# Two units of the modulated projections taken from rows without the norm's factor

## The chip, the cores and the metric

The program runs on one core of one Trainium2 chip. The metric is the device time of one execution in microseconds. Five engines share the work: TensorE (PE, matrix products into PSUM banks; PEld is its weight load), VectorE (DVE), ScalarE (ACT), GpSimd (POOL), and SyncE (SP), which issues most of the transfers.

## The reference, cut to what matters

A residual stream x of 512 tokens by 1024 features goes through mixer a, mixer b, and then a second block, whose entry is the place of this change:

```python
mod = c_act @ ada_w[l] + ada_b[l]
shift, scale, gate = jnp.split(mod, 3, axis=-1)
h = rms_norm_2(x, norm_g[l]) * (1.0 + scale[:, None, :]) + shift[:, None, :]
p = h @ w_in[l]
```

`rms_norm_2` divides each token by the root of its mean square and multiplies by the gain. The modulation (shift, scale, gate) depends on `c` alone, not on the token. So for one unit of 128 columns W of `w_in`, with r the token's factor and g = norm_g * (1 + scale):

p = r * ((x * g) @ W) + shift @ W

The first term can be formed without r, and multiplied by it afterwards; the second is one number for each column. Both versions of the kernel compute the same p.

## The kernel before, in words

The activations lie feature-major: 8 rows (k = 0..7), each a tile of 128 features by 512 tokens. Each product is exact to about fp32 by splitting both sides in a high and a low part: high is a rounded copy written by ScalarE (`HH`, `wh`), low is the difference (`HL`, `wl`). A product of one row with one weight block is three matmuls (low row with high weights, high row with low weights, high with high; `split_product`, L321 to L323). A unit is one block of 128 output columns, that is 8 rows by 3 matmuls into one PSUM bank.

The program is a chain of stages, each a block of one instruction list per engine; between two stages `retire` (L140) clears the semaphores and makes all engines meet. The order within a stage is written out by hand, engine by engine, and kept by semaphores.

Three stages matter:

- Mixer a ends, and mixer b (`attention_layer`, layer b) begins, at 650 to 653 us. This seam already has the form that the change gives to the next seam: the last output units of a write x times the gain (without r) and its high rows; b starts with `raw_two` (L679): two units from those rows, 32 matmuls with the high rows, then 16 with the low rows. In their time the sum of squares is finished (L1000, L691), r is formed (L779, L781), the rows are multiplied by r (L1008), split again (L787, L1017), and the two banks are multiplied by r (`scale_unit`, L997).
- Mixer b's tail: eight output units m = 0..7, 24 matmuls each (L663). VectorE adds the residual (L1188), ScalarE squares each new row (L937), VectorE sums the squares (L309). After the last unit come the sum over features (L756, L758), then Ln and Exp for r (L939, L941), and 20 idle products on TensorE (L761) that keep it at work.
- `modulated_projections` (L1959): units ckv, 4 of qi, ki (0 to 5), and a small one, wi. VectorE forms the scale (L2100) and the eight rows x * scl * r (L2105), ScalarE adds the shift and rounds (L2064), VectorE writes the low rows (L2109). TensorE runs `first_two` (L332): 10 idle products, 32 matmuls with high rows (L339, L340), 16 with low rows (L344); then unit 2 (L321 to L323), in whose middle it makes the sum of squares for the ckv unit's own norm (L2051), which waits for ScalarE's square of bank 0 (`s_lsq`, L2073); then wi, and units 3 to 5. The weights of unit 2 are loaded by SyncE at the start of the stage, rounded by ScalarE (L2060) and their low part is made by GpSimd (L2088).

## Time and profile before

| | us |
|---|---|
| median of 3 runs | 1581.86 |
| lowest and highest of them | 1580.75, 1583.53 |
| the profiled execution, its own time | 1582.13 |
| its span in the trace | 1580.3 |

The span is what the profile shows of the program; 1.8 us of the profiled execution's time lie outside of it. Times in the trace are counted from the span's start. Every row is from that one execution. The granted clock is 1.00 for TensorE at 2.4 GHz and 0.50 at 1.2 GHz. Matmuls overlap, so the distance of two starts, not the length of one, says what a matmul costs.

### The profile page before, as it was taken

How to read it: one execution, taken by the hardware profiler on the slowest of the kernel's cores; microseconds unless marked ns; L12 is line 12 of the kernel's file. 1: busy time of each engine (PE TensorE's matmuls, PEld its weight loads, DVE VectorE, ACT ScalarE, POOL GpSimd, SP SyncE). 2: the span in 40 equal slices, each digit the busy share in tenths (PEclk: the TensorE clock that was granted, in tenths of full speed). 3: DMA queues.
4: the chain of work that ended last, by engine and by line, in shares of the span. 5: the costliest groups of instructions: out<-in, count | busy, mean ns of one | idle time of the engine just before them, and what ended most of it. 6: DMA issues, size and time to landing. Idle time of an engine off the chain costs nothing. (4 is left out here: it accounts for less than half of the span.)

```text
span 1580.3 us, 29922 instructions
## 1 busy us (share of the span) xinstructions
PE 1520.1 (96%) x11664; PEld 1221.9 (77%) x11664; DVE 815.9 (52%) x1931; ACT 783.8 (50%) x1578; POOL 779.6 (49%) x474
## 2 busy tenths in 40 slices
PE   7999999999999999989999999999998998999997
PEld 5888787878888887767777777676777886778886
DVE  5145455464545456835444324189656654274545
ACT  4653637363544545666566643346765532442222
POOL 4734436262625343465654543335777651565651
PEclk9999999999999999999999999999999999999999
DMA  6423132232414130445544214331100001433331
GB/s 155 116 75 111 54 98 80 80 95 65 121 41 122 41 110 28 104 141 152 147 142 127 70 51 105 96 81 54 48 23 3 4 17 29 107 85 103 93 94 54
DMA packets 239413, 131.26 MB, mean 83 GB/s; under 512 B 28678, under 2 KB 233550, under 8 KB 239256
## 3 DMA queue, kind: packets, MB, share of 16 engines
q1 hardware_dynamic: 231736, 114.35, 26.2%
q10 hardware_dynamic: 7536, 14.98, 3.3%
q8 instruction: 94, 1.54, 0.4%
q14 instruction: 47, 0.39, 0.1%
HBM read 126.88 MB, written 2.43 MB: 82 GB/s over the span
## 5 line engine op out<-in xcount | busy, mean ns | idle before, releaser
L1674 POOL TENSOR_TENSOR w_low<-a_w_raw,w_high 128x1024 fp32r<-128x1024 f32 x70 | 172.9, 2472 | 56.7 <-ACT w_high L1560 56.7
L321 PE MATMUL a_proj<-h_low,w_high 128*128 128x512 f32 x488 | 196.4, 402 | 1.2 <-POOL h_low L1692 1.2
L323 PE MATMUL a_proj<-h_high,w_high 128*128 128x512 f32 x488 | 192.0, 393 | 0.0
L322 PE MATMUL a_proj<-h_high,w_low 128*128 128x512 f32 x488 | 191.0, 391 | 0.0
L1687 POOL TENSOR_TENSOR a_sq_low<-a_sq,a_sq_high 128x512 fp32r<-128x512 f32 x48 | 63.0, 1313 | 247.1 <-ACT a_sq_high L1584 247.1
L949 POOL TENSOR_TENSOR w_low<-b_w_raw,w_high 128x1024 fp32r<-128x1024 f32 x40 | 97.4, 2439 | 89.6 <-ACT w_high L772 89.6
L321 PE MATMUL b_proj<-h_low,w_high 128*128 128x512 f32 x288 | 116.1, 403 | 1.4 <-POOL h_low L988 0.8
L323 PE MATMUL b_proj<-h_high,w_high 128*128 128x512 f32 x288 | 113.1, 393 | 0.0
L322 PE MATMUL b_proj<-h_high,w_low 128*128 128x512 f32 x288 | 112.5, 391 | 0.0
L321 PEld LDWEIGHTS a_proj<-h_low,w_high 128*128 128x128 f32 x488 | 91.7, 188 | 23.6 <-issue 1.4
L323 PEld LDWEIGHTS a_proj<-h_high,w_high 128*128 128x128 f32 x488 | 91.7, 188 | 20.7
L322 PEld LDWEIGHTS a_proj<-h_high,w_low 128*128 128x128 f32 x488 | 91.8, 188 | 19.0
L1601 ACT ACTIVATE a_probs<-a_probs,a_stat 128x256 f32<-128x256 f32 x128 | 63.2, 495 | 68.3 <-DVE a_stat L1767 68.3
L1560 ACT ACTIVATE w_high<-a_w_raw 128x1024 fp32r<-128x1024 f32 x70 | 73.3, 1047 | 36.7 <-PE a_proj L323 36.7
L1811 DVE TENSOR_SCALAR a_probs<-a_probs,a_share 128x256 f32<-128x256 f32 x128 | 90.4, 767 | 0.3
L1721 DVE SCALAR_TENSOR_TENSOR a_qk<-a_proj,a_gains,a_rn 128x128 f32<-128x128 f32 (+2 forms) x76 | 39.2, 559 | 83.8 <-ACT a_rn L1570 83.3
L3599 POOL TENSOR_TENSOR merge_w_low<-f_wt,merge_w_high 128x1024 fp32r<-128x1024 f32 x22 | 53.5, 2430 | 34.4 <-ACT merge_w_high L3543 34.4
L321 PE MATMUL a_proj<-a_wv_low,h_high 128*128 128x256 f32 x240 | 68.1, 284 | 0.0
L322 PE MATMUL a_proj<-a_wv_high,h_low 128*128 128x256 f32 x240 | 66.9, 279 | 0.0
L323 PE MATMUL a_proj<-a_wv_high,h_high 128*128 128x256 f32 x240 | 66.8, 278 | 0.0
L2483 POOL TENSOR_TENSOR w_low<-sparse_w_raw,w_high 128x1024 fp32r<-128x1024 f32 x15 | 35.8, 2386 | 60.7 <-ACT w_high L2358 60.7
L321 PEld LDWEIGHTS b_proj<-h_low,w_high 128*128 128x128 f32 x288 | 54.2, 188 | 12.9 <-issue 1.4
(612 smaller groups left out, 4181.4 us busy)
## 6 DMA issues: line engine op xcount, KB each, us to landing
a_w_raw<-in_a_w_in_dram SPq DMA_DIRECT2D x78, 512.0 KB, 3.8
b_w_raw<-in_b_w_in_dram SPq DMA_DIRECT2D x30, 512.0 KB, 4.7
b_ada_w<-in_ada_w_dram ACTq DMA_DIRECT2D x24, 512.0 KB, 3.6
f_wt<-in_w_in_dram SPq DMA_DIRECT2D x18, 512.0 KB, 3.9
sparse_w_raw<-in_w_in_dram SPq DMA_DIRECT2D x17, 512.0 KB, 4.1
a_bias<-scr_a SPq DMA_DIRECT2D x32, 128.0 KB
a_w_raw<-in_a_w_out_dram SPq DMA_DIRECT2D x8, 512.0 KB, 4.2
b_w_raw<-in_b_w_out_dram SPq DMA_DIRECT2D x8, 512.0 KB, 4.2
```

The costliest lines, as they stand in the source:

```text
L321: nc.tensor.matmul(out, lh, rl, start=first, stop=False)
L322: nc.tensor.matmul(out, ll, rh, start=False, stop=False)
L323: return nc.tensor.matmul(out, lh, rh, start=False, stop=last)
L949: nc.gpsimd.tensor_tensor(low(slot_of(b)), raw[:, n % RAW, :, :], high(slot_of(b)), ALU.subtract).then_inc(s_wl, 1)
L1560: nc.scalar.activation(high(slot_of(b)), raw[:, n % RAW, :, :], ACT.Copy).then_inc(s_wh, 1)
L1601: nc.scalar.activation(e, e, ACT.Exp, scale=-1.0, bias=stat[:, own, part, t, h, 0:1], accum_out=stat[:, own, part, t, h, 1:2]).then_inc(s_ ...
L1674: nc.gpsimd.tensor_tensor(low(slot_of(b)), raw[:, n % RAW, :, :], high(slot_of(b)), ALU.subtract).then_inc(s_wl, 1)
L1687: nc.gpsimd.tensor_tensor(sql[:, :], sq[:, u % 2, :], sqh[:, :], ALU.subtract).then_inc(s_sql, 1)
L1721: return nc.vector.scalar_tensor_tensor(out=out, in0=x, scalar=col(gains, u), in1=r, op0=ALU.mult, op1=ALU.mult)
L1811: nc.vector.tensor_scalar(e, e, share[:, part, t, h:h + 1], None, ALU.mult).then_inc(s_pn, 1)
L2483: nc.gpsimd.tensor_tensor(wl[:, slot(u), :, :], wraw[:, u % RAW, :, :], wh[:, slot(u), :, :], ALU.subtract).then_inc(s_wl, 1)
L3599: nc.gpsimd.tensor_tensor(low(b)[:, :, :], raw_of(b), high(b)[:, :, :], ALU.subtract).then_inc(s_wl, 1)
```

## The change

In b's tail, for layer b: VectorE forms the scale and a two-part split of the shift right after the modulation. ScalarE, after each square of rows 2 to 6, also writes the row times the scale into the rows of `T.Y`, and then the high rows 2 to 6 as soon as the last output unit has used the old ones (`s_free`); GpSimd writes the low rows of 2 and 3. The last row's square is left to the next stage. TensorE's sum over the features and its 20 idle products are gone; in their place are 32 small products, the shift (as two columns, high and low) with the weight blocks of the first two units, whose result (2 x 256) ScalarE copies to SBUF.

In `modulated_projections` the rows are taken in the order 2, 3, 4, 5, 6, 0, 1, 7. The first two units are made from the raw rows; between row 3 and row 4 there are two small products, which turn the shift's product into a column per unit, and the sum of squares. ScalarE makes the raw rows 0, 1 and 7, and Ln and Exp. VectorE makes low rows 4, 5, 6, 0, 1, 7, then multiplies eight rows by r; ScalarE adds the shift and rounds; VectorE writes the eight low rows, with the first unit's scaling after the second and the second unit's scaling after the last. ScalarE adds the shift's column to both banks (`s_fixed`) after its eighth high row, and only then squares the ckv bank. The sum of squares of ckv moves within unit 2 from behind the fourth row to behind the sixth. SyncE waits for the two small products before it loads `w_uk`, because those now lie over the shift's rows.

```diff
@@ attention_layer, TensorE
-            pe.wait_ge(s_ln, NQK * PAIRS)
-            pe.wait_ge(s_acc, KT - 2)
-            nc.tensor.matmul(ps_ss[:, :], T.ones, T.rn[:, :], start=True, stop=False)
-            pe.wait_ge(s_nsq, KT)
-            nc.tensor.matmul(ps_ss[:, :], T.ones, sq[:, (KT - 1) % 2, :], start=False, stop=True).then_inc(s_nss, 1)
-            idle_products(nc, T, ps_proj[:, 0, :][:, 0:P], 20)
+            pe.wait_ge(s_mods, 1)
+            pe.wait_ge(s_shift, 2)
+            for j in range(PRE):
+                pe.wait_ge(s_wl, place["next", j] + 1)
+                i = slot_of(("next", j))
+                for k in range(KT):
+                    nc.tensor.matmul(ps_mod[0:2, j * P:(j + 1) * P], T.shift[:, k, :], wl[:, i, k, :], start=(k == 0), stop=False)
+                    mm = nc.tensor.matmul(ps_mod[0:2, j * P:(j + 1) * P], T.shift[:, k, :], wh[:, i, k, :], start=False,
+                                          stop=(k == KT - 1))
+            mm.then_inc(s_shift_row, 1)
@@ attention_layer, ScalarE
-            for m in range(KT):
+            for m in range(KT - 1):
...
-            act.wait_ge(s_nss, 1)
-            nc.scalar.activation(T.rn[:, :], ps_ss[:, :], ACT.Ln, scale=1.0 / D, bias=T.eps[:, 0:1]).then_inc(s_nln, 1)
-            act.wait_ge(s_nln, 1)
-            nc.scalar.activation(T.rn[:, :], T.rn[:, :], ACT.Exp, scale=-0.5).then_inc(s_nr, 1)
+                if m == 2:
+                    act.wait_ge(s_mods, 2)
+                if m >= 2:
+                    nc.scalar.activation(X[:, m, :], L.x_out[:, m, :], ACT.Copy, scale=col(T.scl, m)).then_inc(s_gained, 1)
+            for k in range(2, KT - 1):
+                act.wait_ge(s_gained, k - 1)
+                act.wait_ge(s_free, k + 1)
+                nc.scalar.activation(HH[:, k, :], X[:, k, :], ACT.Copy).then_inc(s_raw_high, 1)
+            act.wait_ge(s_shift_row, 1)
+            nc.scalar.activation(T.shift_rows, ps_mod[0:2, 0:2 * P], ACT.Copy)
@@ attention_layer, GpSimd
+            for k in range(2, 2 + RAW_LOW):
+                pool.wait_ge(s_raw_high, k - 1)
+                nc.gpsimd.tensor_tensor(HL[:, k, :], X[:, k, :], HH[:, k, :], ALU.subtract).then_inc(s_next_low, 1)
@@ attention_layer, VectorE (behind the modulation, ahead of the eight residual sums)
+                nc.vector.scalar_tensor_tensor(out=T.scl[:, 0:KT], in0=T.mod[:, KT:2 * KT], scalar=1.0, in1=T.norm_gain[:, 2, :],
+                                               op0=ALU.add, op1=ALU.mult).then_inc(s_mods, 1)
+                nc.vector.tensor_copy(T.shift[:, :, 0], T.mod[:, 0:KT]).then_inc(s_shift, 1)
+                dve.wait_ge(s_shift, 1)
+                nc.vector.tensor_tensor(T.shift[:, :, 1], T.mod[:, 0:KT], T.shift[:, :, 0], ALU.subtract).then_inc(s_shift, 1)
@@ modulated_projections, SyncE
+            sp.wait_ge(s_shift, 1)
             sp.dma_start(T.wuk, I["w_uk_2"][0].rearrange("c h d -> c (h d)")).then_inc(T.s_kvw, 16)
@@ modulated_projections, TensorE
-            first_two(pe, nc, [ps[:, u, :] for u in range(2)], [wh[:, slot(u)] for u in range(2)],
-                      [wl[:, slot(u)] for u in range(2)], T, s_hh, s_low, s_proj)
+            def raw_two():
+                outs = [(ps[:, u, :], slot(u)) for u in range(2)]
+                for n, k in enumerate(ROWS):
+                    if n >= 5:
+                        pe.wait_ge(s_raw_high, n - 4)
+                    for out, i in outs:
+                        nc.tensor.matmul(out, wl[:, i, k, :], HH[:, k, :], start=(n == 0), stop=False)
+                        mm = nc.tensor.matmul(out, wh[:, i, k, :], HH[:, k, :], start=False, stop=False)
+                    mm.then_inc(s_high_used, 1)
+                    if n == 1:
+                        for u in range(2):
+                            mm = nc.tensor.matmul(ps_mod[:, u:u + 1], T.shift_rows[:, u * P:(u + 1) * P], T.ones[0:2, 0:1], start=True,
+                                                  stop=True)
+                        mm.then_inc(s_shift, 1)
+                        pe.wait_ge(s_sum, 1)
+                        nc.tensor.matmul(ps_ss[:, :], T.ones, T.rn[:, :], start=True, stop=True).then_inc(s_row_ss, 1)
+                for n, k in enumerate(ROWS):
+                    if n >= RAW_LOW:
+                        pe.wait_ge(s_raw_low, n - RAW_LOW + 1)
+                    for out, i in outs:
+                        mm = nc.tensor.matmul(out, wh[:, i, k, :], HL[:, k, :], start=False, stop=(n == KT - 1))
...
-                    if u == PRE and k == 3:
+                    if u == PRE and n == 5:
                         pe.wait_ge(s_lsq, 1)
@@ modulated_projections, ScalarE
+            def raw_row(k):
+                nc.scalar.activation(ht(k), X[:, k, :], ACT.Copy, scale=col(scl, k)).then_inc(s_gained, 1)
+                act.wait_ge(s_gained, ROWS.index(k) - 4)
+                nc.scalar.activation(HH[:, k, :], ht(k), ACT.Copy).then_inc(s_raw_high, 1)
+
+            nc.scalar.activation(sq[:, 0, :], X[:, KT - 1, :], ACT.Square).then_inc(s_last_sq, 1)
+            raw_row(0)
+            raw_row(1)
+            act.wait_ge(s_shift, 1)
+            nc.scalar.activation(shift_of[:, 0:2], ps_mod[:, 0:2], ACT.Copy).then_inc(s_shift_of, 1)
+            act.wait_ge(s_row_ss, 1)
+            nc.scalar.activation(T.rn[:, :], ps_ss[:, :], ACT.Ln, scale=1.0 / D, bias=T.eps[:, 0:1]).then_inc(s_row_ln, 1)
+            act.wait_ge(s_row_ln, 1)
+            nc.scalar.activation(T.rn[:, :], T.rn[:, :], ACT.Exp, scale=-0.5).then_inc(s_row_r, 1)
+            raw_row(KT - 1)
+            split_high(2)
+            for n, k in enumerate(ROWS):
+                act.wait_ge(s_ht, n + 1)
+                act.wait_ge(s_high_used, n + 1)
                 nc.scalar.activation(HH[:, k, :], ht(k), ACT.Identity, bias=T.mod[:, k:k + 1]).then_inc(s_hh, 1)
-            split_high(2)
+            act.wait_ge(s_shift_of, 1)
+            for u in range(2):
+                act.wait_ge(s_scaled, u + 1)
+                nc.scalar.activation(ps[:, u, :], ps[:, u, :], ACT.Identity, bias=col(shift_of, u)).then_inc(s_fixed, 1)
...
                 if kind == "ckv":
-                    act.wait_ge(s_proj, u + 1)
+                    act.wait_ge(s_fixed, u + 1)
@@ modulated_projections, VectorE
-            for k in range(KT):
-                nc.vector.scalar_tensor_tensor(out=ht(k), in0=X[:, k, :], scalar=col(scl, k), in1=T.rn[:, :],
-                                               op0=ALU.mult, op1=ALU.mult).then_inc(s_ht, 1)
+            dve.wait_ge(s_last_sq, 1)
+            nc.vector.tensor_tensor(T.rn[:, :], T.rn[:, :], sq[:, 0, :], ALU.add).then_inc(s_sum, 1)
+            for n, k in enumerate(ROWS):
+                if n >= RAW_LOW:
+                    if n >= 5:
+                        dve.wait_ge(s_raw_high, n - 4)
+                    nc.vector.tensor_tensor(HL[:, k, :], ht(k), HH[:, k, :], ALU.subtract).then_inc(s_raw_low, 1)
+            dve.wait_ge(s_raw_low, KT - RAW_LOW)
+            dve.wait_ge(s_row_r, 1)
+            for k in ROWS:
+                nc.vector.tensor_tensor(ht(k), ht(k), T.rn[:, :], ALU.mult).then_inc(s_ht, 1)
+            for n, k in enumerate(ROWS):
+                if n == 2:
+                    scale_unit(0)
+                dve.wait_ge(s_hh, n + 1)
+                if n < KT - 1:
+                    dve.wait_ge(s_low_used, n + 1)
...
                 nc.vector.scalar_tensor_tensor(out=HL[:, k, :], in0=ht(k), scalar=T.mod[:, k:k + 1], in1=HH[:, k, :],
                                                op0=ALU.add, op1=ALU.subtract).then_inc(s_low, 1)
+            scale_unit(1)
```

## Rows read from the trace of the kernel before

**Rows 1.** The page's part 1: busy time of each engine, its share, instructions.
```profile
PE 1520.1 (96%) x11664; PEld 1221.9 (77%) x11664; DVE 815.9 (52%) x1931; ACT 783.8 (50%) x1578; POOL 779.6 (49%) x474
```

**Rows 2.** Timeline of TensorE at the change: start, length, instructions, idle before.
```profile
965.51 0.40 PE L323 MATMUL b_proj<-h_high,w_high 128*128 128x512 f32 x1
...
968.26 2.74 PE L315 MATMUL b_proj<-pair_ones_r 128*128 128x128 f32 x20
972.15 2.33 PE L315 MATMUL m_proj<-pair_ones_r 128*128 128x128 f32 x10 [1.15 <-PEq L144]
974.28 0.73 PE L339 MATMUL m_proj<-h_high,w_low 128*128 128x512 f32 x1
...
983.88 3.83 PE L344 MATMUL m_proj<-h_low,w_high 128*128 128x512 f32 x16
987.54 0.39 PE L321 MATMUL m_proj<-h_low,w_high 128*128 128x512 f32 x1
...
990.29 1.02 PE L2051 MATMUL m_ss<-m_sq,consts 128*128 128x512 f32 x2
...
993.91 0.40 PE L321 MATMUL m_wi<-h_low,m_wwi_high 128*8 128x512 f32 x1
```

**Rows 3.** Timeline of TensorE at the start of layer b.
```profile
650.17 1.23 PE L315 MATMUL a_scores<-pair_ones_r 128*128 128x128 f32 x10
652.83 0.47 PE L686 MATMUL b_proj<-h_high,w_low 128*128 128x512 f32 x1 [1.43 <-PEq L144]
...
654.76 1.02 PE L691 MATMUL b_ss<-rn,consts 128*128 128x512 f32 x2
...
661.12 3.83 PE L696 MATMUL b_proj<-h_low,w_high 128*128 128x512 f32 x16
665.68 0.47 PE L321 MATMUL b_scores<-h_low,w_high 128*128 128x512 f32 x1 [0.73 <-DVE h_low L1017]
```

**Rows 4.** Windows: stretch, length; PE, PEld, DVE, ACT, POOL busy; granted clock; DMA.
```profile
972.20:979.00 6.80, 6.80 (x21) 5.82 (x22) 6.76 (x12) 5.85 (x9) 0.00 (x0) 0.50 0.94 239
...
1395.70:1398.80 3.10, 1.02 (x6) 0.86 (x5) 3.06 (x2) 2.96 (x4) 2.44 (x2) 1.00 0.00 0
1398.80:1402.30 3.50, 3.50 (x10) 2.73 (x9) 3.47 (x3) 0.00 (x0) 3.50 (x2) 0.51 0.33 75
680.00:683.00 3.00, 0.31 (x5) 0.20 (x4) 1.54 (x3) 2.97 (x4) 0.61 (x1) 1.00 0.56 160
```

**Rows 5.** Timeline of VectorE at the start of layer b.
```profile
657.81 7.12 DVE L1008 TENSOR_TENSOR X<-X,rn 128x512 f32<-128x512 f32 x8
664.86 1.28 DVE L1017 TENSOR_TENSOR h_low<-X,h_high 128x512 fp32r<-128x512 f32 x2
...
670.27 0.69 DVE L997 TENSOR_TENSOR b_proj<-b_proj,rn 128x512 f32<-128x512 f32 x1
```

**Rows 6.** Timeline of ScalarE at the start of layer b.
```profile
652.81 0.63 ACT L774 ACTIVATE b_sq<-Y 128x512 f32<-128x512 f32 x1 [1.86 <-PEq L144]
653.35 0.71 ACT L775 ACTIVATE X<-Y,norm_gain 128x512 f32<-128x512 f32 x1
...
655.81 0.69 ACT L779 ACTIVATE rn<-b_ss,eps 128x512 f32<-128x512 f32 x1 [1.09 <-PE b_ss L691]
656.54 0.63 ACT L781 ACTIVATE rn<-rn 128x512 f32<-128x512 f32 x1
```

**Rows 7.** Instructions by line: duration ns min/median/max, first and last start.
```profile
L1008 DVE TENSOR_TENSOR X<-X,rn x8: 680/682/2900, 657.8 to 664.3; 128x512 f32<-128x512 f32 x8
...
L2088 POOL TENSOR_TENSOR w_low<-m_wt,w_high x4: 2402/2414/5776, 979.5 to 998.5; 128x1024 fp32r<-128x1024 f32 x4
...
L321 PEld LDWEIGHTS m_wi<-h_low,m_wwi_high x8: 88/88/88, 993.7 to 998.5; 128*8 128x8 f32 x8
```

**Rows 8.** Timeline of ScalarE in layer b's last output units.
```profile
960.50 1.06 ACT L772 ACTIVATE w_high<-b_w_raw 128x1024 fp32r<-128x1024 f32 x1 [3.77 <-PE b_proj L323]
```

**Rows 9.** Timeline of VectorE in the modulated stage.
```profile
977.67 4.06 DVE L2109 SCALAR_TENSOR_TENSOR h_low<-Y,mod,h_high 128x512 fp32r<-128x512 f32 x6
```

More of the change, by code:

```diff
@@ L517, in attention_layer @@
         s_op, s_xn = sem("out_proj"), sem("x_new")
+        s_free, s_gained, s_raw_high, s_next_low = (sem(n) for n in ("rows_free", "rows_gained", "raw_rows_high", "next_raw_low"))
+        s_mods, s_shift, s_shift_row = sem("mods_ready"), sem("shift_split"), sem("shift_rows")
         s_last_sq, s_last_row, s_sum, s_raw_low = sem("last_square"), sem("last_raw_row"), sem("sum_added"), sem("raw_rows_low")
@@ L664, in out_product @@
                     mm.then_inc(s_op, 1)
+                elif m == KT - 1:
+                    mm.then_inc(s_free, 1)
             def early_out(k):
@@ L1972, in modulated_projections @@
         ht_own = sb("ht", [P, 2, SEQ])
-        ht = lambda k: T.Y[:, 2 + k, :] if k < KT - 2 else ht_own[:, k - KT + 2, :]
-        ng = T.norm_gain[:, 2, :]
-        scl = sb("scl", [P, LINE])
+        ht = lambda k: T.Y[:, k, :] if k >= 2 else ht_own[:, k, :]
+        scl = T.scl
+        ROWS = [2, 3, 4, 5, 6, 0, 1, 7]
+        shift_of = sb("shift_of", [P, LINE])
+        s_last_sq, s_gained, s_raw_high, s_raw_low = sem("last_square"), sem("rows_gained"), sem("raw_rows_high"), sem("raw_rows_low")
+        s_sum, s_row_ss, s_row_ln, s_row_r = sem("sum_added"), sem("row_ss"), sem("row_ln"), sem("row_r")
+        s_high_used, s_low_used, s_scaled, s_fixed = sem("raw_high_used"), sem("raw_low_used"), sem("scaled"), sem("shifted")
+        s_shift, s_shift_of = sem("shift_product"), sem("shift_kept")
         sq = sb("sq", [P, 1, SEQ])
@@ L2098, in _, with scale_unit @@
         def _(dve):
-            nc.vector.scalar_tensor_tensor(out=scl[:, 0:KT], in0=T.mod[:, KT:2 * KT], scalar=1.0, in1=ng,
-                                           op0=ALU.add, op1=ALU.mult).then_inc(s_modk, 1)
-            dve.wait_ge(s_modk, 1)
-            for k in range(KT):
-                nc.vector.scalar_tensor_tensor(out=ht(k), in0=X[:, k, :], scalar=col(scl, k), in1=T.rn[:, :],
-                                               op0=ALU.mult, op1=ALU.mult).then_inc(s_ht, 1)
-            for k in range(KT):
-                dve.wait_ge(s_hh, k + 1)
+            dve.wait_ge(s_last_sq, 1)
[9 more added lines that the diff above has]
+                nc.vector.tensor_tensor(ht(k), ht(k), T.rn[:, :], ALU.mult).then_inc(s_ht, 1)
+            def scale_unit(u):
+                dve.wait_ge(s_proj, u + 1)
+                nc.vector.tensor_tensor(ps[:, u, :], ps[:, u, :], T.rn[:, :], ALU.mult).then_inc(s_scaled, 1)
+            for n, k in enumerate(ROWS):
+                if n == 2:
+                    scale_unit(0)
+                dve.wait_ge(s_hh, n + 1)
+                if n < KT - 1:
+                    dve.wait_ge(s_low_used, n + 1)
+                else:
+                    dve.wait_ge(s_proj, 2)
                 nc.vector.scalar_tensor_tensor(out=HL[:, k, :], in0=ht(k), scalar=T.mod[:, k:k + 1], in1=HH[:, k, :],
                                                op0=ALU.add, op1=ALU.subtract).then_inc(s_low, 1)
+            scale_unit(1)
             dve.wait_ge(s_latg, 16)
@@ L2125, in _ @@
                 elif kind == "qi":
-                    dve.wait_ge(s_proj, u + 1)
+                    if u < 2:
+                        dve.wait_ge(s_fixed, u + 1)
+                    else:
+                        dve.wait_ge(s_proj, u + 1)
                     nc.vector.tensor_copy(v(out)[:, :, ::-1], v(src)).then_inc(s_take, 1)
@@ L3727, in build @@
         T.causal = part("causal")
+        T.scl, T.shift_rows = sb("scl", [P, LINE]), T.Y[0:2, 0, 0:2 * P]
+        T.shift = ctx.enter_context(nc.sbuf_tensor("shift", [P, KT, 2], F32R))
         a, b = layer_a_space(T, I), layer_b(T, I)
```

14 lines of the change are left out of this document (10 added, 4 removed).

## The prediction

> **What bounds the kernel now.** I read the page first: TensorE is busy for 96% of the span [rows 1], so time is won only where TensorE waits or runs slowly. Then TensorE's timeline at this seam. The last product of layer b starts at 965.51, the first of the modulated stage at 974.28, and unit 2 at 987.54 [rows 2]. With one matmul every 0.229 us (16 in 3.83, the last 0.39 long [rows 3]) the 48 matmuls of the first two units are 11.0 us of work, yet 21.8 us pass between b's last slot (965.74) and unit 2. The rest is the norm's chain, a meeting of the engines (1.15), 30 idle products, and a slow clock: the windows show 0.50 granted from 972.20 to 979.00 [rows 4], so 1.2 GHz in place of 2.4; matmuls 0.43 apart cost some 3.2 us there. From unit 2 on TensorE has no gap: unit 2 ends at 993.91, when wi starts [rows 2]. This start of wi is my marker: behind it the stage is a solid row of products, and what the marker moves by, the time moves by. Marker before: 993.91, or 21.76 after the stage's first instruction at 972.15.
>
> The seam between layers a and b has the form that the change introduces here, so its rows [rows 3, 5, 6] are my template. From the last idle product's end there TensorE waits 1.43, keeps its clock (the first 8 matmuls take 1.93), and starts unit 2 at 12.85 after the stage's start, having waited 0.73 for VectorE.
>
> **The stage's start.** Removed: the sum of squares, Ln, Exp and 20 idle products (968.26 to 971.00). Added: 32 small products (128 x 2 weights, 128 columns). The nearest rows are the idle products, also 128 columns wide: ten in 1.23 us, 0.107 apart (the last about 0.27 long) [rows 3], and 0.129 in the group at 968.26 [rows 2]. I take 0.107: 3.4 us, so they end at 969.3; the bounds are 4.1 us, and, as these have two columns of weights where the idle ones have 128, something below: half of 0.107, so 1.7 us. ScalarE then copies 2 x 256; its nearest operation (128 x 512, 0.63 [rows 6]) is larger, I take 0.4: 969.7. The meeting adds 1.15 [rows 2]: start 970.9, that is 1.25 earlier than 972.15.
>
> The Trainium skill (TensorE: Matmul & The Clock Gate, LDWEIGHTS) says that a weight load's time goes by its columns, and (Back-to-back issue gap) gives 134 cycles for 128 columns, 56 ns. The rows agree in direction on the load: 88 ns with 8 columns [rows 7]. By that figure, an estimate, the 32 products would take 1.8 us and the stage would start 1.6 us earlier than in my sum.
>
> The other additions to b's tail are covered. ScalarE's five row operations of 0.71 and five of 0.63 fall in idle time of 3.77 us per unit [rows 8], the last high row some 0.7 us behind its use, at 966; GpSimd's two low rows follow its last weight block and end near 967.3, and VectorE's last sum at 967. All are ready before 969.3. VectorE's three or four tiny operations lie in an idle stretch of several us.
>
> **The stage, in time after its first instruction.** In the template the sum of squares starts at 1.93, Ln at 2.98, Exp at 3.71, and VectorE's eight products with r at 4.98 [rows 3, 5, 6]. What differs:
>
> - Two small fp32 products, two matmuls each, ahead of the sum of squares: at most 0.107 each, 0.4. Ln at 3.4, Exp from 4.1 to 4.75. ScalarE's square, rows 0 and 1 and the copy are done at 3.3, so they don't delay it.
> - Row 7 comes only after Exp: gain and rounding, 5.4 and 6.0. VectorE, in order, writes low row 7 (6.05 to 6.75) before it may multiply. So the eight products with r start at 6.75, 1.8 later than in the template.
> - They take 7.12 in the template, because GpSimd's low part of unit 2's weights falls in it: seven 0.68 long, one 2.90 [rows 5, 7]. Here ScalarE rounds these weights at 6.0 to 7.1, and GpSimd starts at 7.1, again within the eight. End: 13.9.
> - TensorE meanwhile: 8.29 for the high pass [rows 3] plus 0.4, 3.66 for the low one: done at 12.35.
> - The low rows now carry the shift, 0.665 apart (six in 4.06 [rows 9]). The first is ready at 14.6. TensorE waits 2.25 and starts unit 2.
> - The first unit's scaling (0.6) sits between low rows 1 and 2: row 2 is ready at 16.55, TensorE would want it at 16.0: 0.55 more.
> - Scaling of unit 1 follows all eight low rows: 13.85 + 8 x 0.665 + 0.6 = 19.8, end 20.45 [rows 5]. ScalarE adds the shift to bank 1, rounds wi's weights, and only then squares bank 0: 0.6 + 0.2 + 0.6, so 21.9. TensorE needs this square behind row six of unit 2, at 14.6 + 0.55 + 6 x 0.687 = 19.3. It waits 2.6 us. Before, TensorE did not wait at this place [rows 2].
> - From the sum of squares to the marker it was 3.62 [rows 2] with four rows; with two it is 2.25. Marker at 24.15.
>
> Marker before 21.76, now 24.15: 2.4 later in the stage, less 1.25 at its start: **+1.15 us**. What the norm's chain, the idle products and the slow clock cost before is given back to a longer chain ScalarE, VectorE, ScalarE. Without the three waits (5.4 us) it would win 4.25.
>
> Nothing is late behind the marker: unit 3's weights are rounded after ckv's Exp, at 25, and low at 27.5; wi's products keep TensorE until 29.6. SyncE's new wait stands behind its weight loads and is over at 2.3, so I price it at nothing; late, it would delay only loads for the sparse stage, over 30 us off.
>
> **The clock.** TensorE idles 1.6, 2.25 and 2.6 us. The trace shows both outcomes of such gaps: after some 2.1 us idle at 1395.7 the clock was 0.51 for 3.5 us, after 2.7 us idle at 680 it stayed 1.00 [rows 4]. One fall costs 1.75 us where TensorE is the bound, that is after the third gap; after the second it is hidden by the third. I put it at 0.4, so +0.7. The profiled execution (1582.13, span 1580.3) lies 0.27 above the median of the runs: 1582.13 + 1.15 + 0.7 = 1583.98, and on the scale of the median 1583.7.
>
> **Rivals.**
>
> - *The gain comes through* (faster). If ScalarE's square of bank 0 or VectorE's low rows were not late, 4.25 go: 1577.6. It decides at a square before 19.3. Against it: the code fixes the order, and each duration has a row. With only the cheap small products (1.7 us) and GpSimd not stopping VectorE (2.2 off), unit 2 would start at 12.4 and the square come at 19.7 against 16.6: net -2.8, 1579.1, still within the bound.
> - *GpSimd is the one stopped.* The same operation took 5.78 once, and 2.41 else [rows 7], beside VectorE's low rows with the shift. If it must wait out the eight products, and then the low rows, unit 2's weights are ready at about 20: the marker is at 26.5, +3.5: 1585.4. Against it stands the template's 2.90, where VectorE is the one that waits. The Trainium skill (SBUF — State Buffer, section SBUF: two separate sides) describes one port pair that VectorE and GpSimd lock in turn, the other fully blocked; the trace agrees with both of these rows.
> - *The clock falls at the seam*, after the small products and the meeting, as before. Then 8 matmuls and the sum of squares run at 0.43 and 0.86: 2.3 later, and the whole chain with them: 1.15 + 2.3 = +3.45, 1585.3. For: before, 30 small products and 1.15 us idle ended in 0.50 [rows 2, 4]. Against: the template's seam, 1.43 idle, kept the full rate. With a fall behind the third gap too: +5.2, 1587.
>
> **Chances.** Forecast 0.55; the part way case (1579 to 1581) 0.10; gain in full 0.10; GpSimd stopped 0.09; clock at the seam 0.16. What a measurement can tell from no change is about 0.2%, 3.2 us: so faster 0.10, same 0.65, slower 0.25. Range 1579.0 to 1586.5: it leaves out the full gain and the double fall.
>
> **What would show it.** In the profile after: the stage's first matmul at 970.9 and its clock; the eight products with r beginning 6.75 later; unit 2 starting 14.6 later, released by a VectorE low row; TensorE idle for 2.6 us before the sum of squares in unit 2, released by ScalarE's square. If that gap is missing, I am wrong to the fast side; if the clock column reads 0.5 in the stage, or GpSimd's low weights take over 4 us, to the slow side.

## The result, and the profile after

The changed kernel takes 1588.33 us (median; 1585.15 to 1594.02), the kernel before 1582.56 us in the same rounds (1579.13 to 1590.86): ratio 1.0035, 95% interval [1.0024, 1.0047], so 5.5 us slower, where 1.85 us were forecast. The time lies above the range's upper end of 1586.5. The profiled execution has a span of 1584.8 us (1580.3 before).

Part 1 of the page after (busy time, share, instructions): TensorE's share is still 96% [rows 1].

```profile
PE 1523.2 (96%) x11668; PEld 1223.1 (77%) x11668; DVE 822.7 (52%) x1942; ACT 794.6 (50%) x1598; POOL 778.5 (49%) x476
```

TensorE's timeline of the changed kernel at the seam (start, length, instruction, count, idle before it and its releaser). The row at 968.42 is layer b's last product, the two with `shift` are the first and the last of the 32 small ones, 996.80 is the marker, the start of wi [rows 2]:

```profile
968.42 0.39 PE L323 MATMUL b_proj<-h_high,w_high 128*128 128x512 f32 x1
968.64 0.22 PE L764 MATMUL b_mod<-w_low,shift 128*2 128x128 f32 x1
...
970.50 0.22 PE L765 MATMUL b_mod<-w_high,shift 128*2 128x128 f32 x1
972.33 0.47 PE L2061 MATMUL m_proj<-h_high,w_low 128*128 128x512 f32 x1 [1.60 <-PEq L144]
...
974.34 0.60 PE L2066 MATMUL m_mod<-consts,Y 2*128 2x1 f32 x4
974.87 1.12 PE L2070 MATMUL m_ss<-rn,consts 128*128 128x512 f32 x2
...
981.34 3.82 PE L2075 MATMUL m_proj<-h_low,w_high 128*128 128x512 f32 x16
987.35 0.47 PE L321 MATMUL m_proj<-h_low,w_high 128*128 128x512 f32 x1 [2.19 <-DVE h_low L2204]
...
994.46 1.12 PE L2109 MATMUL m_ss<-m_sq,consts 128*128 128x512 f32 x2 [1.15 <-ACT m_sq L2152]
...
996.80 0.40 PE L321 MATMUL m_wi<-h_low,m_wwi_high 128*8 128x512 f32 x1
```

From layer b's last product to the stage's first instruction it is 972.33 - 968.42 = 3.91 us, in place of 6.64 [rows 2]; from there to the marker 24.47 in place of 21.76. Together 28.38 after and 28.40 before. In this pair of traces the seam costs nothing, and yet the marker stands at 996.80 in place of 993.91: the 2.9 us are there already when layer b's last product starts. They are not made at the seam. Counted against the same products of before, the changed kernel is 1.17 us behind at 40 us (a fall of the clock at 25.3 cost 1.6), loses 1.62 in layer a between 40 and 640, and 0.1 from there to the seam. Behind the marker it gains 0.56 up to 1405, where the two traces have their falls of the clock in different places, and loses another 2.08 in the merge stage, from 1405 on. Together that is the 4.4 us between the two spans.

VectorE's timeline there. The group at 979.42 begins the eight products with r (template [rows 5]), 986.47 the low rows with the shift:

```profile
978.69 0.69 DVE L2185 TENSOR_TENSOR h_low<-Y,h_high 128x512 fp32r<-128x512 f32 x1 [2.02 <-ACT h_high L2124]
979.42 5.32 DVE L2189 TENSOR_TENSOR Y<-Y,rn 128x512 f32<-128x512 f32 x5
...
986.47 1.40 DVE L2204 SCALAR_TENSOR_TENSOR h_low<-Y,mod,h_high 128x512 fp32r<-128x512 f32 x2
```

And ScalarE's: Exp at 976.75, then row 7 (977.29), the rounding of unit 2's weights (978.57), and far below the square of bank 0 (993.82), for which TensorE's sum of squares at 994.46 waits:

```profile
976.75 0.63 ACT L2134 ACTIVATE rn<-rn 128x512 f32<-128x512 f32 x1
977.29 0.71 ACT L2122 ACTIVATE Y<-X,scl 128x512 f32<-128x512 f32 x1
...
978.57 1.04 ACT L2118 ACTIVATE w_high<-m_wt 128x1024 fp32r<-128x1024 f32 x1
...
993.82 0.59 ACT L2152 ACTIVATE m_sq<-m_proj 128x512 f32<-128x512 f32 x1
```

The rows show the chain of the prediction: VectorE waits 2.02 us for row 7's high part, multiplies from 7.09 us after the stage's start on, and TensorE's unit 2 waits 2.19 us for its first low row. The first five of these products take 5.32 us, as GpSimd's low part of unit 2's weights (979.69, 2.69 us long) falls among them. Two windows of the changed kernel (TensorE, weight loads, VectorE, ScalarE, GpSimd busy; granted clock) show the gap and the half clock behind it:

```profile
985.10:987.40 2.30, 0.11 (x2) 0.08 (x1) 2.30 (x5) 2.27 (x4) 0.00 (x0) 1.00 0.89 250
987.90:991.40 3.50, 3.50 (x10) 2.72 (x9) 3.50 (x6) 0.66 (x1) 0.00 (x0) 0.52 1.10 286
```

### The profile page after: what moved, and what is told of

Read it like the earlier page. It is cut to its first block and busy times, and to the rows that moved or that the text cites. A ratio compares the mean times of both kernels' runs of the same rounds, so it can differ in the third digit from the quotient of the medians.

```text
span 1584.8 us, 29987 instructions
## 1 busy us (share of the span) xinstructions
PE 1523.2 (96%) x11668; PEld 1223.1 (77%) x11668; DVE 822.7 (52%) x1942; ACT 794.6 (50%) x1598; POOL 778.5 (49%) x476
```

## The experiments

Each run was timed beside the kernel before, in four sets (e0 to e3, e4 to e7, e8 to e10, e11), in which that kernel had medians of 1582.98, 1582.46, 1582.50 and 1582.91 us. Most runs have 11 or 12 executions, e5 has six and e6 seven; each has one trace. "Layer a" is the time from one product of layer a to the same product late in it (40.21 to 640.10 in the span of before), "merge" the same from 1405.21 to 1570.60, "seam" that from layer b's last product to wi's first. In brackets behind "seam": how long the clock was at half rate there.

| run | what it is | ratio, 95% interval | layer a | merge | seam |
|---|---|---|---|---|---|
| before | | | 599.89 | 165.39 | 28.40 (6.8) |
| after | | 1.0035 [1.0024, 1.0047] | 601.51 | 167.47 | 28.38 (3.4) |
| e0 | after, once more | 1.0042 [1.0028, 1.0056] | 601.68 | 167.50 | 28.39 (none) |
| e1 | before, tensors moved 128 bytes | 1.0022 [1.0008, 1.0037] | 601.67 | 167.50 | 27.51 (3.4) |
| e2 | after, tensors in place | 0.9997 [0.9984, 1.0011] | 599.87 | 165.39 | 28.40 (3.4) |
| e3 | after, early square | 1.0016 [1.0004, 1.0028] | 601.71 | 167.51 | 27.09 (3.4) |
| e4 | in place, early square | 0.9999 [0.9982, 1.0015] | 599.93 | 165.39 | 26.94 (3.4) |
| e5 | before, moved 64 | 1.0041 [1.0026, 1.0057] | 603.46 | 165.15 | 27.41 (3.4) |
| e6 | before, moved back 64 | 1.0036 [1.0014, 1.0057] | 602.05 | 167.45 | 27.48 (3.4) |
| e7 | e4 with idle products | 0.9997 [0.9983, 1.0012] | 599.87 | 165.40 | 25.98 (none) |
| e8 | e4 with another order | 0.9984 [0.9967, 1.0000] | 599.88 | 165.39 | 24.65 (none) |
| e9 | before, merge's tensors moved 128 | 1.0010 [0.9996, 1.0024] | 599.95 | 167.49 | 26.81 (3.4, part of it idle) |
| e10 | before, layer a's moved 128 | 1.0009 [0.9996, 1.0021] | 601.39 | 165.40 | 26.35 (none) |
| e11 | e8 once more | 0.9980 [0.9963, 0.9998] | 600.08 | 165.39 | 24.67 (none) |

**e0, the changed kernel unedited.** 

> The changed kernel unedited, as a yardstick beside the other three. All theories expect the ratio on record, 1.0035 (some 5 us over the kernel before). In the first profile the seam itself cost nothing (the small unit wi starts 28.4 us after layer b's last product in both kernels), and half of the 4.4 us came in the merge stage, whose matmuls of 512 columns were 231.7 ns apart and not 228.7. If that is a property of the program (theory LAYOUT), this second profile shows 231 to 232 again; if it was that one execution (theory CHANCE), it shows 228 to 230.

It was slower again, by 1.0042. Its TensorE rows at the seam:

```profile
966.84 0.40 PE L323 MATMUL b_proj<-h_high,w_high 128*128 128x512 f32 x1
...
992.88 1.12 PE L2109 MATMUL m_ss<-m_sq,consts 128*128 128x512 f32 x2 [2.21 <-ACT m_sq L2152]
...
995.23 0.40 PE L321 MATMUL m_wi<-h_low,m_wwi_high 128*8 128x512 f32 x1
```

Here the clock did not fall at the seam, and the seam is as long as with the fall: 28.39. The wait before the sum of squares is 2.21 us long here and 1.15 in the first trace. So a fall behind the gap costs nothing in this order; it only eats into the wait behind it. That second profile also has the 1.8 us in layer a and the 2.1 us in the merge stage again, so that these do not come from one execution.

**e1, the move alone.** The change adds two tensors of 64 bytes a partition, `scl` and `shift`, behind the shared constants, and everything allocated later lies 128 bytes further on: it starts 192 bytes behind a multiple of 256 where it was 64. This kernel is the one before with just that:

```
         T.causal = part("causal")
+        T.scl = sb("scl", [P, LINE])
+        T.shift = ctx.enter_context(nc.sbuf_tensor("shift", [P, KT, 2], F32R))
```

> The kernel before with nothing but the two new small tensors of the changed kernel allocated (scl and shift, 64 bytes each per partition, unused), so that every tensor of every stage behind them moves by 128 bytes. Theory LAYOUT (the loss is the moved tensors, above all in the merge stage): slower than before by 2.5 to 5 us, ratio 1.0015 to 1.003, and 231 to 232 ns between the merge stage's matmuls. Theory SEAM (the loss is the longer chain at the start of the modulated stage): ratio within 1.0008 of 1, 228 to 229 ns. Theory CHANCE (falls of the clock at other places): the same as SEAM for the ratio, pace anything.

1.0022: not one instruction differs, and the kernel is 3.5 us slower. What is slower is TensorE's products. Groups by form in the merge stage (1405 to 1570) of the kernel before (line, operation, out<-in, count, busy us, mean ns of one):

```profile
L323 PE MATMUL z<-h_high,merge_w_high 128*128 128x512 f32 x40 | 15.7, 392 | 0.0
...
L322 PE MATMUL z<-h_high,merge_w_low 128*128 128x512 f32 x40 | 15.6, 389 | 0.0
L322 PE MATMUL z<-f_y_high,merge_w_low 128*128 128x512 f32 x40 | 15.6, 389 | 0.0
L322 PE MATMUL z<-h_high,f_w_low 128*128 128x512 f32 x40 | 15.5, 388 | 0.0
```

and of the changed kernel:

```profile
L322 PE MATMUL z<-h_high,f_w_low 128*128 128x512 f32 x40 | 15.8, 396 | 0.0
L322 PE MATMUL z<-f_y_high,merge_w_low 128*128 128x512 f32 x40 | 15.8, 395 | 0.0
...
L323 PE MATMUL z<-h_high,merge_w_high 128*128 128x512 f32 x40 | 15.7, 391 | 0.0
L322 PE MATMUL z<-h_high,merge_w_low 128*128 128x512 f32 x40 | 15.6, 391 | 0.0
```

`h_high` and `merge_w_high`, which lie where they lay, go together as before (392 and 391 ns, with `merge_w_low` 389 and 391). Where one operand is a moved tensor, `f_w_low` or `f_y_high`, the mean goes from 388 to 396 and from 389 to 395. (The order of the groups in the two views differs, as they stand by busy time.) Worked out from the starts of all products of 512 columns in that stage that follow each other directly (some 680), the pace goes from 228.74 to 231.75 ns, and to 231.80 in e0, e1, e3 and 231.81 in e9; in e2 it is 228.73.

**e2, the change without the move.** The changed kernel, with its two new tensors in space that is there: `shift` where `eps` was, `eps` in the unused fourth line of the norm's gains, `scl` in the unused end of the modulation's line.

```
-        T.eps = sb("eps", [P, LINE])
+        T.shift = ctx.enter_context(nc.sbuf_tensor("shift", [P, KT, 2], F32R))
         T.norm_gain = sb("norm_gain", [P, 4, KT])
+        T.eps = T.norm_gain[:, 3, :]
...
-        T.scl, T.shift_rows = sb("scl", [P, LINE]), T.Y[0:2, 0, 0:2 * P]
-        T.shift = ctx.enter_context(nc.sbuf_tensor("shift", [P, KT, 2], F32R))
+        T.scl, T.shift_rows = T.mod_lines[:, MODS:MODS + KT], T.Y[0:2, 0, 0:2 * P]
```

> The changed kernel with its two new tensors put where the kernel before has room (shift in the 64 bytes of eps, eps and scl in unused columns of norm_gain and mod), so that all other tensors lie as before. Theory LAYOUT: the ratio falls from 1.0035 to 1.000 to 1.0015, and the merge stage's pace to 228 to 229 ns. Theory SEAM: the ratio stays at 1.003 to 1.004.

0.9997: the changed kernel's instructions, all of them, cost nothing that can be measured once nothing is moved. Against e0 in the same rounds this is 7.1 us, where the two stages' rows account for 3.9. The 3.2 us left over are about as much as the two intervals, 2.2 us to either side each, allow for; no row shows them.

**e3, the early square.** The wait for the square of bank 0, taken away by order: ScalarE squares it right behind the shift's addition to that bank, and no longer behind the second bank's.

```
                 nc.scalar.activation(ps[:, u, :], ps[:, u, :], ACT.Identity, bias=col(shift_of, u)).then_inc(s_fixed, 1)
+                if u == 0:
+                    act.wait_ge(s_fixed, 1)
+                    nc.scalar.activation(sq[:, 0, :], ps[:, 0, :], ACT.Square).then_inc(s_lsq, 1)
```

> The changed kernel, in whose modulated stage ScalarE squares the ckv bank right after its own correction and no longer after that of the second bank. By my sum TensorE's wait ahead of the sum of squares in unit 2 goes (2.6 us at full clock; 1.15 us in the profile, where a slow clock hid the rest): 1 to 2.6 us faster than the changed kernel, ratio to before 1.002 to 1.003. Under LAYOUT the rest of the loss stays; if the wait was the loss (SEAM), most of the 5 us goes only if the clock's fall at this place goes with it.

TensorE's rows: the sum of squares (994.70) no longer waits.

```profile
969.86 0.39 PE L323 MATMUL b_proj<-h_high,w_high 128*128 128x512 f32 x1
...
994.70 1.02 PE L2109 MATMUL m_ss<-m_sq,consts 128*128 128x512 f32 x2
...
996.95 0.40 PE L321 MATMUL m_wi<-h_low,m_wwi_high 128*8 128x512 f32 x1
```

The seam is 27.09, 1.3 shorter, with a fall of the clock in it (3.4 us from 989.8) that is no longer hidden. The ratio, 1.0016 beside 1.0042, goes the same way by 0.0026, but the two intervals touch.

**e4, both.** 

> The changed kernel with both edits at once: the new tensors take space that was already there, so that every other tensor lies where it lay before (as in the earlier run without the move), and the sum of squares of the latent keys gets its square right after the shift of the first bank (as in the earlier run with the early square). Those two alone read 0.9997 and 1.0016 of the kernel before, against 1.0042 for the changed kernel itself. Theory A (the two costs are independent and add): 1.0042 - 0.0045 - 0.0026 = 0.9971, some 1578.4 us beside 1583.0, the first version faster than both kernels. Theory B (the wait before the sum of squares was only visible because the rest was late, or the early square lands on another wait): no gain over the kernel without the move, 0.9997, 1582.5 us. In the trace A shows the first matmul of the wi columns 2 to 3 us nearer to layer b's last product than 28.4 us.

0.9999, with the interval [0.9982, 1.0015]: theory B's 0.9997 fits, theory A's 0.9971 doesn't. The sum was made from e3's ratio, 0.0026 or 4.1 us, and the seam in the traces gives a third of that. They show it at 26.94, 1.5 us shorter than in e2, so the square did come through there. Taken off e2's time, these 1.5 us would give 0.9988, which lies in the interval as well: the time of e4 can't tell the seam's gain from none. e4's trace shows something else, too: in layer b TensorE stood for 2.79 us with nothing that releases it (idle before, "issue"), and within that time, at 705.4, the clock fell to half:

```profile
706.71 1.09 PE L629 MATMUL b_turned<-consts,b_probs 128*128 128x128 f32 x4 [2.79 <-issue]
```

The same instruction has the same 2.79 in e5's trace, where the clock fell 0.4 us behind it, and in none of the other twelve. Against the kernel before, what follows it lies 5.6 us (e4) and 4.6 us (e5) later than what came ahead of it. One execution with such a stall says nothing of the edit.

**e5 and e6, other distances.** In e5 the kernel before has one 64-byte tensor ahead of all later ones; in e6 `eps` goes into the norm's gains, as in e2, and everything behind lies 64 bytes earlier.

> The kernel before, with one unused tensor of 64 bytes a partition allocated behind the constants, so that every later tensor lies 64 bytes further on (the move of 128 bytes alone read 1.0022). No instruction differs. The merge stage's tensors lie at 64 in a block of 256 bytes before, at 192 after the move of 128, and at 128 here. Theory A (the pace of TensorE depends on the place within 256 bytes, and only some places are slow): a pace in the merge stage (span 1405 to 1570) of either 228.7 or 231.8 ns a product, as the place decides, and a time to match: 1583 or 1586.5 us. Theory B (any place other than the one the kernel was written with is worse, by how far things moved): between, 230.2 ns and 1584.7 us. Theory C (the slower pace is no matter of places, but came with the runs): 228.7 ns, 1583 us.

> The kernel before, with the 64 bytes of the eps tensor saved (eps goes into the unused fourth line of the norm gains), so that every tensor from the norm gains on lies 64 bytes earlier: the merge stage's tensors lie at 0 in a block of 256 bytes, in place of 64. No instruction differs but for that operand. Theory A (places within 256 bytes decide): 228.7 or 231.8 ns in the merge stage; if the best place is the start of a block, at most 228.7 and a time at or under 1583 us. Theory B (any move away costs): about 230 ns, 1584.7 us.

By the ratios both are slower than before. By stages it is neither theory pure. The merge stage is at 231.71 ns and +2.06 us with the move back, and at 228.37 ns and -0.24 us with the move of 64; layer a is slower in all three other places, by 2.16, 3.57 and 1.7 us. So the merge stage answers to the place, not to the distance (theory A holds there, with two of four places slow), and the place that is good for one stage is the worst of the four for the other. (e6 also moves the norm's gains, `rn` and the modulation's lines, so its place, 0, is shown less cleanly than the others. And e5's ratio is 6.5 us, of which its two stages show 3.3; whether the stall in its trace is in its other executions too isn't known.)

In layer a the groups say which products these are. The dearest ones with data from `a_wv_low`, a moved tensor, and weights from `h_high`, which stays, in the kernel before and in e5 (mean length 284 and 288 ns):

```profile
L321 PE MATMUL a_proj<-a_wv_low,h_high 128*128 128x256 f32 x240 | 68.1, 284 | 0.0
```

```profile
L321 PE MATMUL a_proj<-a_wv_low,h_high 128*128 128x256 f32 x240 | 69.0, 288 | 0.0
```

Worked out from the starts, the 753 products of 256 columns that follow each other there, all with data from `a_wv_high` or `a_wv_low`, are 117.1 ns apart before, 119.4 in e1, 120.3 in e6 and 121.3 in e5: +1.72, +2.40 and +3.20 us, nearly all of what the stage loses. The 1,665 of 512 columns, most of them with neither operand moved, change by +0.14, -0.09 and +0.48 us.

**e9 and e10, one stage's tensors at a time.** An unused tensor of 128 bytes ahead of the merge stage's own tensors (its edit is shown), or ahead of layer a's; nothing else moves.

```
+        sb("moved", [P, 32])
         wt = sb("wt", [P, 3, KT, P])
```

> The kernel before, with an unused tensor of 128 bytes a partition at the head of the merge stage's own tensors alone: only these lie 128 bytes further on. Against the kernel before, the traces of all four kernels with the move of 128 bytes lose 1.6 to 1.8 us in layer a (span 40 to 640) and 2.1 us in the merge stage (1405 to 1570), and those without it lose 0.0. Theory A (the pace follows the stage's own tensors): 231.8 ns a product in the merge stage in place of 228.7, +2.1 us there, nothing in layer a: 1.0013, 1584.6 us. Theory B (it hangs on the shared tensors, rn and the modulation lines, which lie ahead of them): 228.7 ns, no change, 1.0000.

The merge stage's first and last products in the kernel before, and in e9; both have one clock fall right behind the first row:

```profile
1397.79 0.47 PE L321 MATMUL f_p<-f_y_low,merge_w_high 128*128 128x512 f32 x1 [2.08 <-POOL f_y_low L3618]
...
1568.85 0.39 PE L323 MATMUL f_p<-f_merged_high,f_w_high 128*128 128x512 f32 x1
```

```profile
1399.56 0.47 PE L321 MATMUL f_p<-f_y_low,merge_w_high 128*128 128x512 f32 x1 [1.87 <-POOL f_y_low L3619]
...
1572.73 0.40 PE L323 MATMUL f_p<-f_merged_high,f_w_high 128*128 128x512 f32 x1
```

171.06 us before, 173.17 in e9: +2.11, and nothing in layer a (+0.06).

> The kernel before, with an unused tensor of 128 bytes a partition at the head of layer a's own tensors alone. Theory A (the pace follows the stage's own tensors): +1.7 us between 40 and 640 of the span, nothing in the merge stage, 1.0011, 1584.2 us. Theory B (it hangs on the shared tensors): no change, 1.0000. If both this and the move in the merge stage show their part, they make 3.8 us together, the 3.5 us that the move of everything cost (1.0022).

e10's product of layer a that stands at 40.21 in before, the one that stands at 640.10 there, and the seam:

```profile
40.90 0.39 PE L322 MATMUL a_scores<-h_high,w_low 128*128 128x512 f32 x1
...
642.29 0.40 PE L322 MATMUL a_proj<-h_high,w_low 128*128 128x512 f32 x1
...
967.73 0.40 PE L323 MATMUL b_proj<-h_high,w_high 128*128 128x512 f32 x1
...
974.38 1.30 PE L315 MATMUL m_proj<-pair_ones_r 128*128 128x128 f32 x10 [1.15 <-PEq L144]
...
994.08 0.40 PE L321 MATMUL m_wi<-h_low,m_wwi_high 128*8 128x512 f32 x1
```

601.39 us in place of 599.89: +1.5, and nothing in the merge stage (+0.01). Each stage's pace follows that stage's own tensors. In the time of the whole, 1.0010 and 1.0009, each is too small to be told from none; the two stages' losses add up to 3.6 us, beside 3.9 in e1.

The last three rows show the old seam with the clock up: 26.35 us. The six traces with the old seam read 26.35 to 28.40, the shortest with no fall of the clock, the longest, which is the one that the prediction read, with 6.8 us at half rate. A fall costs the old order time; the changed one reads 28.38 to 28.40 with a fall and without.

**e7, idle products in the gap.** e4 with work for TensorE ahead of unit 2:

```
+                if u == PRE:
+                    idle_products(nc, T, ps[:, u % 4, 0:P], 16)
                 for n, k in enumerate(ROWS):
```

> As the version with both edits, with 16 idle products of 128 columns (0.137 us each, 2.2 us) put into the bank of unit 2 ahead of its first wait, so that TensorE has work in the gap of 2.2 us between the second bank's last low product and unit 2. Theory A (the gap is what lets the granted clock fall right behind it, in all four traces of the changed kernels so far, 3.4 us at half clock = 1.7 us each): the clock stays up behind the gap, and the time is 1.5 us or so lower than without the idle products, 0.9961. Theory B (the clock falls anyway, there or elsewhere, or the gap isn't what decides): no difference from the version without, 0.9971.

```profile
967.29 0.40 PE L323 MATMUL b_proj<-h_high,w_high 128*128 128x512 f32 x1
...
983.90 1.90 PE L315 MATMUL m_proj<-pair_ones_r 128*128 128x128 f32 x16
...
993.27 0.41 PE L321 MATMUL m_wi<-h_low,m_wwi_high 128*8 128x512 f32 x1
```

The gap is filled but for 0.36 us, the clock stays up, and the seam is 25.98. But 0.9997 is neither theory's time (both started from the 0.9971 that e4 missed), and beside e4's 0.9999 it decides nothing. One trace of each is no proof that the filled gap kept the clock: with the gap open it stayed up in e0 as well.

**e8 and e11, the chain shortened.** On top of e4, row 7's low part goes between the fifth and sixth product with r, the rounding of unit 2's weights behind the second high row with the shift, and the first unit's scaling one low row later.

```
-            split_high(2)
             for n, k in enumerate(ROWS):
+                if n == 2:
+                    split_high(2)
                 act.wait_ge(s_ht, n + 1)
...
-                if n >= RAW_LOW:
+                if RAW_LOW <= n < KT - 1:
...
-            dve.wait_ge(s_raw_low, KT - RAW_LOW)
+            dve.wait_ge(s_raw_low, KT - 1 - RAW_LOW)
             dve.wait_ge(s_row_r, 1)
-            for k in ROWS:
+            for n, k in enumerate(ROWS):
+                if n == 5:
+                    dve.wait_ge(s_raw_high, 3)
+                    nc.vector.tensor_tensor(HL[:, ROWS[-1], :], ht(ROWS[-1]), HH[:, ROWS[-1], :], ALU.subtract).then_inc(s_raw_low, 1)
+                    dve.wait_ge(s_raw_low, KT - RAW_LOW)
...
-                if n == 2:
+                if n == 3:
                     scale_unit(0)
```

> The version with the tensors kept in place and the early square, with the order on VectorE and ScalarE changed at the seam: the products with the norm's factor start as soon as the factor is there, with the last raw row's low part put between the fifth and the sixth of them instead of ahead of all; ScalarE splits unit 2's weights behind the second of the new high rows instead of ahead of the first; the first bank is scaled behind the third of the new low rows instead of the second. So far VectorE starts its products 7.1 us after the stage's start and is the last to come for unit 2 (TensorE idle 2.2 us). Theory A (this serial chain is what eats the gain at the seam): the products start about 5 us after the stage's start, the gap of 2.2 us ahead of unit 2 goes, and wi starts about 25.2 us behind layer b's last product in place of 27 (28.4 before): some 2 to 3 us faster than before, 0.998, 1579.5 us. Theory B (the split of unit 2's weights, now later, is the next to be late, or GpSimd's part of it slows VectorE in another place): the gap stays above 1 us, and the time is that of the version without it, 0.9998, 1582.5 us.

e8's TensorE:

```profile
967.76 0.40 PE L323 MATMUL b_proj<-h_high,w_high 128*128 128x512 f32 x1
...
971.68 0.47 PE L2061 MATMUL m_proj<-h_high,w_low 128*128 128x512 f32 x1 [1.60 <-PEq L144]
...
985.38 0.47 PE L321 MATMUL m_proj<-h_low,w_high 128*128 128x512 f32 x1 [0.86 <-DVE h_low L2210]
...
990.07 1.02 PE L2109 MATMUL m_ss<-m_sq,consts 128*128 128x512 f32 x2
...
992.41 0.40 PE L321 MATMUL m_wi<-h_low,m_wwi_high 128*8 128x512 f32 x1
```

Its VectorE (the products with r are `Y<-Y,rn` and `m_ht<-m_ht,rn`), and GpSimd's low part of unit 2's weights:

```profile
976.85 3.10 DVE L2195 TENSOR_TENSOR Y<-Y,rn 128x512 f32<-128x512 f32 x5 [0.83 <-ACT rn L2134]
979.87 0.68 DVE L2193 TENSOR_TENSOR h_low<-Y,h_high 128x512 fp32r<-128x512 f32 x1
980.59 3.39 DVE L2195 TENSOR_TENSOR m_ht<-m_ht,rn 128x512 f32<-128x512 f32 x2
983.90 0.68 DVE L2195 TENSOR_TENSOR Y<-Y,rn 128x512 f32<-128x512 f32 x1
984.50 2.06 DVE L2210 SCALAR_TENSOR_TENSOR h_low<-Y,mod,h_high 128x512 fp32r<-128x512 f32 x3
```

```profile
980.28 2.55 POOL L2169 TENSOR_TENSOR w_low<-m_wt,w_high 128x1024 fp32r<-128x1024 f32 x1 [10.71 <-ACT w_high L2118]
```

The products start 5.2 us after the stage's first instruction, the gap before unit 2 is 0.86 in place of 2.18, and the seam 24.65 in place of the changed kernel's 28.38. The clock did not fall at this seam. Against the old seam it is 3.7 us less than in the profiled kernel before (28.40, the clock low for 6.8 us), 2.7 less than the mean of the six, and 1.7 less than with the clock up (26.35). The first five products took 0.62 us each, the two that fell into GpSimd's 2.55 us took 3.39 together. At 0.62 each they would take 2.15 less, more than the gap of 0.86; that this would close it is an estimate. The Trainium skill (SBUF — State Buffer, section SBUF: two separate sides) says that VectorE and GpSimd lock one pair of ports in turn; these rows agree.

By the rows this is theory A: the gap is under 1 us, and the seam even shorter than the 25.2 expected. By the time of e8 alone, A's 0.998 and B's 0.9998 both lie in the interval, which is why it was run again:

> The version with the new order at the seam once more, unedited, since its first interval, 0.9967 to 1.0, ends at no change. Theory A (the 3.8 us that its trace shows between layer b's last product and the start of wi, 24.6 us against 28.4, come through in the time of the whole): 0.998, 1579.5 us, and with the first run together an interval below 1. Theory B (the chance falls of the clock and stalls swallow it, or the first median was lucky): 0.9995 or more, 1582 us.

0.9984 [0.9967, 1.0000], then 0.9980 [0.9963, 0.9998], theory A's time both times: faster than the kernel before by some 3 us, 0.2%, with one interval that touches 1 and one that lies just under it. The ratios of the changed kernel, 1.0035 and 1.0042, lie 8 to 10 us above these, of which the move back is the larger part.

## Why the prediction was wrong

**The step that failed** is the one that carries the marker to the end: "what the marker moves by, the time moves by", and with it the sum "1582.13 + 1.15 + 0.7", which takes every other stage at its old length. The two new tensors were read for what the instructions on them cost ("The other additions to b's tail are covered") and not for where they push everything else. That is the larger part of the measured loss: layer a +1.62 us and the merge stage +2.08, 3.7 us of the 5.5. The prediction had this term at nothing, without a reason. e1 shows it by itself (+3.5), e2 takes it away (the ratio is 0.9997 without it), e9 and e10 show that it belongs to each stage's own tensors.

**The seam's sum**, +1.15 us, was worked out against the profiled kernel before, and there it measured 0.0: 1.48 us too little gained at the stage's start, 0.32 too little lost in the stage. It also took that trace's 6.8 us of low clock for a fixed part of the old seam. Against the old seam with the clock up (26.35 in e10) the changed one costs +2.0, against the mean of the six old ones (27.3) +1.1; that this last number is the forecast one is luck, as the start, sized too small, and the fall, taken as fixed, offset each other. Term by term:

- *The stage's start.* Forecast 1.25 earlier, measured 2.73 (3.91 against 6.64). The small products were mis-sized: 32 in 2.1 us (968.64 to 970.72), 0.06 apart, in place of 3.4. The idle products, taken as the nearest row, were the wrong neighbour. The estimate of 1.8 us from the Trainium skill (TensorE: Matmul & The Clock Gate, Back-to-back issue gap) was nearer: the spacing measured here is within 4 ns of its 56. That figure is the page's for a product by itself; the same section gives about 81 ns for a stream of weight loads and products of 128 columns, which these rows, with two columns of weights, lie under.
- *Products with r* from 6.75 on: 7.09. *Unit 2* at 14.6, after 2.25 of idle time: 15.02, after 2.19, released by a VectorE low row. Right.
- *The wait for the low row behind the first unit's scaling*, 0.55: 0.20 (e0).
- *The wait before the sum of squares*, 2.6: 2.21 where no fall hides in it (e0). Right, by its cause as well (e3: the order on ScalarE alone took it away).
- *The marker* 24.15 after the stage's start: 24.47.
- *SyncE's new wait and ScalarE's copy* at nothing and 0.4: nothing was seen of the first, the copy took 0.37.

**The clock**, +0.7: wrong in form. A fall behind the second gap came in the first trace (987.8, 3.4 us long) and cost nothing, as the prediction said it might ("after the second it is hidden by the third"); behind the third gap none was seen in after, e0 or e2.

**The rivals.** *The gain comes through* did not happen as the change was written, because the square and the first low row came late; e3, e4 and e8 make it true by order, step by step, and it is worth 3.7 us against the seam of the changed kernel. *GpSimd is the one stopped* did not occur: its low part took 2.69 us, and VectorE's five products beside it 5.32 in place of the 3.10 that e8 shows for them. *The clock falls at the seam*, ahead of the sum of squares, did not occur either.

**What stays open.** The move's 3.7 us and the seam's 0 to 2 us add up to the measured 5.5, but e2's and e1's intervals are each some 2 us wide on either side, so that the split of what is left can't be told. Nor is it known what in the place of a tensor slows the products, which of the merge stage's tensors it is (in layer a the rows point at `a_wv_high` and `a_wv_low`), or what the 2.79 us of "issue" in two of fourteen traces were; such events of 5 us are of the size of the spread of the times (1578 to 1591 for the kernel before).

## What to carry to other kernels

Ahead of a forecast on a kernel that TensorE fills, ask of each new tensor where it stands in the allocation and what lies behind it. Put it last or into space that is free, and time once the old kernel with nothing but the allocation changed: the move can cost more than the change it came with.

Where a chain passes between two engines, look at what each does in between that the chain doesn't need: four operations put elsewhere in their order (a square earlier; a low row, a rounding and a scaling later) shortened a seam that gained nothing by 3.7 us. And a wait that the clock's fall hides behind will show that fall as soon as the wait is gone: e3 and e4 have one in a seam of 27.0, e7 has none in one of 26.0.

Before a row of the old kernel is taken as its fixed cost, look whether the clock fell in it. The same old seam took 26.35 to 28.40 us in six traces, and the prediction's came from the longest.

## What the runs showed of the hardware

- TensorE's pace depends on where in memory its operands lie. Products of 512 columns in the merge stage, by where its tensors start behind a multiple of 256 bytes: 0: 231.7 ns; 64: 228.7; 128: 228.4; 192: 231.8. Layer a, in the same order: 602.05, 599.89, 603.46 and 601.6 us for the same instructions; there it is the products of 256 columns with data from a moved tensor, 120.3, 117.1, 121.3 and 119.4 ns apart. (The place 0 is e6's, which moves a few shared tensors too.) The lengths of VectorE's, ScalarE's and GpSimd's work did not change with it.
- Products with two columns of weights and 128 columns of data start 0.06 us apart; the idle ones at these seams, with 128 columns of weights, nearly all 0.106 to 0.114 at the full clock.
- TensorE can stand for 2.79 us with nothing in the trace that it waits for, at the same place of the program in two of fourteen executions (e4, e5).
